# A decoder-layer kernel: state-space decays as repeated rows by DMA, z gated through tanh, four samples' scores in one pass of the array

## Time and profile before

| | us |
|---|---|
| median of three runs | 853.85 (851.89 to 855.59) |
| the profiled execution's own time | 847.97 |
| its span in the trace | 846.4 |
| PE busy | 780.7 (92%) |
| DVE busy | 364.7 (43%) |
| ACT busy | 304.5 (36%) |
| POOL busy | 98.5 (12%) |
| DMA moved | 219.68 MB, mean 260 GB/s |

### The profile page before, as it was taken

How to read it: one execution, slowest core, us unless ns; L and a number is a source line. 1 busy time by engine, 2 the same in 40 slices (tenths; PEclk the granted TensorE clock), 3 DMA queues, 4 the chain that set the end, 5 groups by cost and what they waited for, 6 DMA issues and landing times.

```text
span 846.4 us, 12511 instructions
## 1 busy us (share of the span) xinstructions
PE 780.7 (92%) x4573; PEld 546.0 (65%) x4573; DVE 364.7 (43%) x845; ACT 304.5 (36%) x733; POOL 98.5 (12%) x156
## 2 busy tenths in 40 slices
PE   3798979999999899898999999999779999999997
PEld 3375757787776687677887778888534444344434
DVE  3355636675675066375999511112301232222203
ACT  1223216675566256463977100101312222112213
POOL 4321021121200212512001100000010000000000
PEclk9899989999999999999999989999779999999999
DMA  9796353778675712227998995562859999999992
GB/s 294 245 353 216 100 162 118 260 231 299 208 274 180 244 39 78 87 70 212 403 279 255 358 357 183 158 240 100 305 190 423 420 421 420 422 419 421 422 419 97
DMA packets 93532, 219.68 MB, mean 260 GB/s; under 512 B 11792, under 2 KB 67672, under 8 KB 78980
## 3 DMA queue, kind: packets, MB, share of 16 engines
q1 hardware_dynamic: 78850, 181.71, 59.0%
q0 software_dynamic: 7984, 31.87, 11.4%
q10 hardware_dynamic: 6634, 5.25, 2.0%
HBM read 207.58 MB, written 13.22 MB: 261 GB/s over the span
## 4 chain that ended last, share of the span: by engine, by line
PE 66%; DMA 11%; SPq 9%; ACT 5%; DVE 3%; issue 3%; POOL 1%; POOLq 1%; ACTq 0%; DVEq 0%
PE bank L1622 17%; PE bank L1927 9%; PE bank L1848 7%; SPq L549 5%; PE bank L1949 5%; PE bank L1555 4%; DMA out_ssm_sample<-arena 4%; PE bank L1856 4%; PE bank L1618 3%; DMA arena<-in_w_down 3%; PE bank L1830 3%; PE bank L1968 2%; SPq L530 2%; PE bank L1678 2%; DMA out_k_prompt<-arena 1%
## 5 line engine op out<-in xcount | busy, mean ns | idle before, releaser
L1622 PE MATMUL bank<-h_normed,weight_ring 128*128 128x264 f32 x1024 | 243.2, 395 | 10.1 <-ACT arena L894 6.0
L1622 PEld LDWEIGHTS bank<-h_normed,weight_ring 128*128 128x128 f32 x1024 | 195.3, 194 | 48.1 <-ACT arena L894 6.4
L1927 PE MATMUL bank<-arena,h_normed 128*64 128x512 f32 x176 | 79.0, 603 | 0.0
L1848 PE MATMUL bank<-y_T,weight_ring 128*128 128x264 f32 x256 | 58.7, 392 | 0.0
L1927 PE MATMUL bank<-weight_ring,h_normed 128*64 128x512 f32 x192 | 56.3, 594 | 0.6 <-ACT h_normed L1031 0.6
L1848 PEld LDWEIGHTS bank<-y_T,weight_ring 128*128 128x128 f32 x256 | 49.4, 194 | 8.6
L1488 DVE SCALAR_TENSOR_TENSOR x_residual<-bank,modulation,x_residual 128x256 f32<-128x256 f32 x64 | 28.8, 484 | 57.9 <-PE bank L1968 57.9
L1481 DVE TENSOR_TENSOR arena<-arena,bank 128x512 f32<-128x512 f32 x8 | 8.7, 1087 | 104.5 <-PE bank L1927 104.5
L1555 PE MATMUL bank<-identity,arena 128*128 128x128 f32 (+5 forms) x236 | 32.2, 277 | 16.7 <-ACT arena L830 9.3
L1555 PEld LDWEIGHTS bank<-identity,arena 128*128 128x128 f32 (+5 forms) x236 | 26.7, 148 | 27.8 <-issue 22.8
L981 ACT ACTIVATE arena<-conv_out,expanded 128x128 f32<-128x128 f32 x128 | 38.3, 388 | 12.7 <-DVE arena L1364 11.7
(11 more groups left out here) (354 smaller groups left out, 1213.2 us busy)
## 6 DMA issues: line engine op xcount, KB each, us to landing
weight_ring<-in_w_in SPq DMA_DIRECT2D x36, 1024.0 KB, 6.5
weight_ring<-in_w_mod SPq DMA_DIRECT2D x22, 1024.0 KB, 9.3
arena<-in_w_up SPq DMA_DIRECT2D x14, 1024.0 KB, 19.9
weight_ring<-in_w_gate SPq DMA_DIRECT2D x14, 1024.0 KB, 20.0
arena<-in_w_down SPq DMA_DIRECT2D x11, 1024.0 KB, 26.7
weight_ring<-in_w_up SPq DMA_DIRECT2D x10, 1024.0 KB, 18.6
arena<-in_state_ssm POOLq DMA_DIRECT2D x8, 1024.0 KB, 9.1
out_ssm_sample<-arena POOLq DMA_DIRECT2D x8, 1024.0 KB, 9.9
```

The costliest lines, as they stand in the source:

```text
L1622: ins = mm(ps[:, 0:T], w, hT[:, c, :], start=c == 0, stop=c == KD - 1)
L1848: ins = mm(ps[:, 0:T], w, yT[:, c, :], start=c == 0, stop=c == NXB - 1)
L1927: ins = mm(banks[i][BLK * e:BLK * e + BLK, :], xg[:, 4 * h + c, BLK * e:BLK * e + BLK], ws[e][:, c, :], start=h == 0 and c == 0, stop=h == ...
```

## The change

- **Scores of samples.** `qbd` shrinks to 32 columns per (sample, key pair), `ss` acts only at c = 3 and c = 7, and then does four samples together, each as a 32-column tile of its own. Samples are taken in the order TURN; five key buffers instead of two. `modt` of an odd turn moves behind the next turn's `s`.
- **Decays.** `ab` leaves PE and PSUM. ACT stores the sums to memory at `fd` and reads each block's four rows back, repeated over 128 partitions (256 KB), into one of three buffers, three blocks ahead. DVE subtracts from that buffer, ACT takes the exponential of it. `ab`, `wt` (the weighing) and `y` become one pipeline of 16 steps.
- **z.** ACT takes `tanh(z/2)` of all 264 columns; DVE does `(tanh+1)*z`, which is twice `z*sigmoid(z)`. The factor 2 goes away in the norm, whose scale gets 1/4, and `g_ssm` is halved.
- **Squares** of y times gate move from DVE to ACT; the pair sums follow one step later.
- **d_skip** comes as rows by a DMA in `load_small` and two DVE copies in `fd`; the job `exp` goes. POOL loads `x2` and `dq` ahead of scaling `xd`, and DVE uses them at `fs`.

```diff
-            jobs += [("s", c, 0), ("s", c, 1), ("sc", c, 0), ("sc", c, 1), ("xbc", 3 * c), ("sk", c, 0), ("sk", c, 1),
+            jobs += [("s", c, 0), ("s", c, 1)]
+            if c and c % 2 == 0:
+                jobs += [("modt", 1 + c // 2)]
...
-        jobs += [("bs", 0), ("bs", 1), ("exp",)]
-        jobs += [("bt", a) for a in range(2)]
...
+        jobs += [("bs", 0), ("bs", 1)] + [("bt", a) for a in range(2)]
+        jobs += [("ab", n) for n in range(3)] + [("xs", 0, g) for g in range(4)] + [("cb", 0), ("wt", 0), ("z", 4)]
+        fill = {0: [("z", 5)], 1: [("xs", 1, g) for g in range(4)] + [("z", 6)], 2: [("z", 7)],
+                3: [("s1", g) for g in range(4)] + [("ct", 0)], 4: [("cb", 1), ("z", 8)], 5: [("z", 9), ("ct", 1)],
+                6: [("z", 10)], 7: [("z", 11), ("ct", 2)], 8: [("z", 12)], 9: [("z", 13)], 10: [("ct", 3)],
+                11: [("z", 14)], 12: [("ct", 4)], 13: [("z", 15)], 14: [("ct", 5)]}
+        for n in range(16):
+            jobs += [("wt", n + 1)] * (n < 15) + [("y", n // 8, n % 8)] + [("ab", n + 3)] * (n < 13) + fill.get(n, [])
...
+                sp.dma_start(exo[:, NXB:NXB + SH], t["d_skip"].to_broadcast([128, SH])).then_inc(late_in, 16)
...
+            def load_sums(n):
+                act.dma_start(raw[n % 3], ac_d[n // 8:n // 8 + 1, 512 * (n % 8):512 * (n % 8) + 512].to_broadcast([128, 512]))\
+                   .then_inc(ac_full[n % 3], 16)
...
                 elif k == "so":
+                    if j[1] == 0:
+                        act.wait_ge(cf_out, 32)
+                        for n in range(3):
+                            load_sums(n)
...
                 elif k == "ab":
+                    n, b = j[1], j[1] % 8
+                    if n >= 8:
+                        act.wait_ge(ac_full[n % 3], 16 * (n // 3 + 1))
...
+                        link(fn(ce[:, b % 3, :], raw[n % 3], ACT.Exp), et_ready)
+                    act.wait_ge(seg_ready, n + 1)
+                    link(fn(wd[:, n % 3, :], wd[:, n % 3, :], ACT.Exp), seg_exp)
+                    if n + 3 < 16:
+                        load_sums(n + 3)
+                elif k == "y" and j[1] == 1:
+                    b = j[2]
+                    act.wait_ge(yz_ready, b + 1)
+                    fn(u[:, 2 * b:2 * b + 2, 0:NP], yT[:, 2 * b:2 * b + 2, 0:NP], ACT.Square).then_inc(yz_sq, 1)
...
-                    link(fn(zb[:, i, :], ps[:, 0:NP], ACT.Silu))
-                    release(act, fn(zsS[:, i, :], ps[:, NP:T], ACT.Silu), j)
+                    if i >= 2:
+                        read_out(act, ("z", i - 2))
+                    link(fn(zth[i % 2], ps[:, 0:T], ACT.Tanh, scale=0.5), z_tanh)
...
+                elif k == "z":
+                    ps, i = filled(dve, j), j[1]
+                    dve.wait_ge(z_tanh, i + 1)
+                    v.scalar_tensor_tensor(zb[:, i, :], zth[i % 2][:, 0:NP], 1.0, ps[:, 0:NP], ALU.add, ALU.mult)
+                    ins = v.scalar_tensor_tensor(zsS[:, i, :], zth[i % 2][:, NP:T], 1.0, ps[:, NP:T], ALU.add, ALU.mult)
...
-                        mm(sbank[:, 0:257], qbd[:, o:o + 128], ktb[:, b % 2, m, :], start=b == 0 and m == 0, stop=False)
+                        for i in range(b - 3, b + 1):
+                            r, o = 32 * (TURN[i] // 2), 32 * (4 * TURN[i] + m)
+                            mm(sbank[r:r + 32, 0:257], qbd[:, o:o + 32], ktb(i)[:, m, :], start=b == 3 and m == 0, stop=False,
+                               tile_position=(0, r), skip_group_check=True)
```

198 lines of the change are left out of this document (89 added, 109 removed), and 3 rows, old and new, of the table fill.

## The result

The changed kernel takes 842.61 us (839.77 to 844.53, 4 runs) where the kernel before takes 853.34 (4 runs): ratio 0.9893, interval 0.9857 to 0.993. That is 10.7 us won, and not the 28 forecast; the time lies above the upper end of the range (839). The profiled execution took 841.94 us with a span of 840.3, against 847.97 and 846.4.

The account below looks back on a forecast made before the run. PE was taken as the bound, with 66% of the chain of waits. Terms: 10.7 + 18.2 + 0.7 - 0.5 - 0.7 = 28.4 us, so 853.85 - 28 = 826 us; 8-in-10 range 817 to 839.

Parts of the forecast that it names:

- Samples' scores, 10.7: Loop over c: tiled `ss` saves 10.3 us and moved `modt` 1.9, less 1.5 for DVE; gain 10.7 us.
- State-space stage, 18.2: From 297.46 to `fs`: 91.8 us less 71.1 of work that stays and 2.5 of PE waiting; gain 18.2 us.
- The walk through the steps: State-space stage: PE waits 0.7 us behind step 10, 1.1 at step 13, 0.2 at 15, 0.5 at start: 2.5.
- sum of 4.7 a step: Chunk 1 of the state-space stage: DVE's work in a step with a z, 4.7 us, under PE's 4.85.
- the first (DVE becomes the bound): State-space stage: DVE's work makes it 80 us instead of 73.6; gain 19, kernel 835 us; chance 0.20.
- What is won ahead of 389 us moves them to the left and is kept: Samples' states and experts, behind the stage: they begin at PE's marks, so the whole earlier gain stays.
- Rival 2: Samples' states: gate weights push two state transfers back 4 to 5 us each; kernel 836 us; chance 0.08.
- Clock of `fs`, 0.7: Start of `fs`: smaller holes before it may avoid the low clock; gain 0.7 us, ends 0 and 1.4.
- `d_skip`, 0.5: SP's queue ahead of the router weights `fd` waits for: one more DMA costs 0.5 us, ends 0 and 3.3.
- Three loads, 0.7: At `sx`: ACT issues three loads before copying the first `so`; cost 0.7 us, ends 0 and 2.5.
- rival 3: State-space stage: repeated rows land late; 28 us eaten at 18.5 us landing, 869 us at 22; chance 0.03.
- rival 4: Score tiles run one after another (back 10.3 us), or tanh and exp alternate through table loads: about 836; chance 0.06.

Follow-up runs that it names:

- e0: The changed kernel run again unaltered, as yardstick for the other runs: 840.1 us, stage 80.4 us.
- e4: Changed kernel without GpSimd's three scalings of xd, the products reading another tile of the same size: stage 76.5 us.
- e17: Changed kernel with SyncE's weight loads held until the four final-state stores have landed: fourth store's issue 0.73 us, stage 79.9 us.
- e2: Changed kernel with the four final-state stores issued by GpSimd behind its loads of states, instead of by ScalarE: ratio 0.9869.
- e5: Kernel before with the scores' part alone (tiled `ss`, 32-column operand, five key buffers, moved `modt`): 840.41 us against 850.35.
- e15: Changed kernel with each step's fill (tile of z, transposed tail) put ahead of subtraction and exponentials: stage 77.9 us.

## Why the prediction was wrong, step by step

**Samples' scores, 10.7: right.** 9.5 in the loop, 9.9 us for this part alone (850.35 to 840.41). A call took 1.88 us. A matmul of it, and two groups of the weight loads (PEld) behind it:

```profile
187.22 0.41 PE L1715 MATMUL bank<-arena,y_T 128*32 128x257 f32 x2
```
```profile
187.46 0.12 PEld L1715 LDWEIGHTS bank<-arena,y_T 128*32 128x32 f32 x2
187.47 0.12 PEld L1715 LDWEIGHTS bank<-y_T 128*32 128x32 f32 x2
```

The loads of the four tiles start within 0.02 us of each other and run while the matmuls before are in flight, though all use the same 128 rows. The Trainium skill, "TensorE: Matmul & The Clock Gate", Part 3, says that weight loads overlap with matmuls in flight only when the row group differs; this trace does not agree, and what the prediction drew from that rule, tiles that pay for their loads one after another, did not come.

**State-space stage, 18.2: the step that failed.** The sentence was "In the new order a block's sums, exponential and weighing are done one to three steps before PE wants them", and behind it the stalls of 2.5 us. Of the 18.2, the 2.0 of `exp` lie ahead of `cb` and came; of the other 16.2 the stage brought 1.8 in the first profile and 6.8 in e0. The removed work was sized rightly, and the term that failed is PE's waiting, put at 2.5 us with the full clock behind it. In the first profile it is 12.1 us of holes and 4.7 of matmuls drawn out at a lower clock, in e0 8.2 and 3.6 (the second figure is what the stage holds beyond its holes and the 68.5 us of work, 71.0 less 2.5).

Two things are in it. The walk through the steps had 0.7 us behind step 10 and 1.1 at step 13, and 2.67 and 1.87 were measured; this part stands without the scalings too (2.68 and 1.86 in e4, whose stage of 76.5 is 5.5 us over the predicted 71.0: 3.65 of holes, 1.9 of low clock). Its cause wasn't isolated; four attempts only moved it.

The other, which I did not have at all, is the hold by GpSimd's scalings, 3.8 us in e0 and 8.8 in the first profile by comparison with e4. The prices of DVE's instructions were read from rows in which they ran undisturbed (0.69 in the earlier trace rows). Their sum of 4.7 a step was even too high, 3.7 in the trace; it said nothing of when each is ready.

Of the rivals, the first (DVE becomes the bound) had 80 us for the stage counted from 297.46, that is 77.4 from `cb`, and 835 for the kernel; 80.4 and 85.3, and 840 and 843, were measured. It had half the reason: DVE is late, but not by the amount of its work.

**"What is won ahead of 389 us moves them to the left and is kept": wrong.** `fs` was 10.3 us earlier, `pb` 6.7. Rival 2 had this place and 4 to 5 us, but by state transfers; it is the issue of a store, which stands on ACT ahead of the first products and is held by the weight loads (e17, e2). Once that is mended the states' transfers take part of it back, as rival 2 had it: `pb` comes 99 to 103 us behind the first products instead of 97 to 98. Both errors together leave the state-space part next to nothing: e5 and e0 have the same median.

**Clock of `fs`, 0.7:** 1.6 came (9.01 to 7.41), just over the upper end of 1.4. **`d_skip`, 0.5:** `fd` starts at 39.28 instead of 38.56, 0.7. **Three loads, 0.7:** 1.9 us (`so` to `so` 21.6 for 19.7); the prediction said that the later wait would swallow the first, and did not see that a hole of 2.21 us puts the next tiles at the lower clock, 16.09 us instead of 14.41. **Repeated rows late (rival 3), table loads (rival 4):** neither; the loads landed in 3.0 to 5.7 us and no table load stands between the first tanh and `fs`. The Trainium skill, "ScalarE: Activation LUTs", Table sets, has tanh in the set of exp, and the trace agrees.

## What to carry to other kernels

When work is moved so that two engines overlap that did not before, their durations can't be taken from the old trace: look for pairs of VectorE instructions with SBUF inputs and GpSimd instructions, keep the GpSimd ones short (quarters: 0.2 to 1.5 us of hold instead of 3, though here hardly less waiting on PE), let them meet work that reads PSUM, or let them meet an instruction that PE doesn't wait for next, as in e15. An issue of a DMA is an instruction in its engine's queue and lasted 7.8 to 9.6 us here beside 1 MB loads; put nothing urgent behind it, and don't let large loads be freed at the moment when small stores start. And follow the gain to the next engine that has to start: here 10.3 us at one mark were 4.8 at the next.

## What the hardware did that I had not expected

- A VectorE product of 128x512 took 3.35 and 3.75 us instead of 0.69, four subtractions 3.70 instead of 0.87, beside a GpSimd product of 3.62 us; beside four pieces of 1.2 us, 0.85 to 2.40.
- The same program had a stage of 85.3 us in one execution and 80.4 in another, by which of two subtractions a scaling held.
- The issue of a 256 KB store on ScalarE's queue took 7.8 to 9.6 us beside 1 MB weight loads, and 0.39 to 0.80 once these were held back, with the DMA engines as full.
- Sixteen matmuls in four column groups of 32, 257 columns each, took 1.88 us, with the weight loads under way beside matmuls of the same rows.
